# First experts: the bias row loaded once as 64 bytes a partition and spread over the rows by a VectorE transpose

## The reference, cut to what matters

```
u   = xb @ w1[e] + b1[e]                  # xb [rows, 1024], w1 [1024, 2048], b1 [2048]
glu = min(u[:, 0::2], 7)
lin = clip(u[:, 1::2], -7, 7)
act = glu * sigmoid(1.702 * glu) * (lin + 1)
y   = act @ w2[e] + b2[e]                 # w2 [1024, 1024]
```

## Time and profile before

| | us |
|---|---|
| median of 3 runs | 2942.95 |
| lowest, highest | 2941.94, 2943.54 |
| profiled execution | 2945.77 |
| its span on the core | 2944.0 |

### The profile page before, as it was taken

How to read it: one execution, slowest core, us unless ns; L and a number is a source line. 1 busy time by engine, 2 the same in 40 slices (tenths; PEclk the granted TensorE clock), 3 DMA queues, 4 the chain that set the end, 5 groups by cost and what they waited for, 6 DMA issues and landing times. The chain is left out here.

```text
span 2944.0 us, 49984 instructions
## 1 busy us (share of the span) xinstructions
PE 2274.4 (77%) x21092; PEld 1351.8 (46%) x21092; DVE 1044.5 (35%) x1860; ACT 741.9 (25%) x1812; POOL 116.7 (4%) x135
## 2 busy tenths in 40 slices
PE   4978798579999988888889946994897377574781
PEld 3944366424433333333333415884564246463660
DVE  2244554412222211122122224225565764543114
ACT  3123454111111101001011102223565414321231
POOL 0000000000000000000000010000000111000001
PEclk8988799779999999899999967997998588795995
DMA  5256501189999999999999943210000000303973
GB/s 213 97 228 218 233 1 65 60 343 364 370 406 395 401 404 402 401 399 401 396 399 400 405 165 139 99 37 5 1 1 1 1 1 8 122 15 152 417 294 116
DMA packets 148324, 631.12 MB, mean 214 GB/s; under 512 B 30788, under 2 KB 62532, under 8 KB 94856
## 3 DMA queue, kind: packets, MB, share of 16 engines
q1 hardware_dynamic: 118584, 580.48, 50.4%
q0 software_dynamic: 8352, 30.41, 2.8%
q10 hardware_dynamic: 21168, 17.06, 1.8%
HBM read 593.55 MB, written 34.37 MB: 213 GB/s over the span
## 5 line engine op out<-in xcount | busy, mean ns | idle before, releaser
L2024 PE MATMUL psum<-w,x 128*32 128x512 f32 x5696 | 674.9, 623 | 124.7 <-DMA w<-in_w_mlp 112.3
L2024 PEld LDWEIGHTS psum<-w,x 128*32 128x32 f32 x5696 | 183.3, 113 | 553.2 <-issue 398.3
L2175 DVE TENSOR_TENSOR u<-psum,x 128x512 f32<-128x512 f32 x89 | 61.5, 691 | 824.0 <-PE psum L2024 824.0
L2033 PE MATMUL psum<-w,act_turned 128*32 128x256 f32 x5696 | 330.8, 385 | 3.9 <-DVE act_turned L2184 3.6
L731 PE MATMUL psum<-high 128*128 128x512 f32 (+3 forms) x832 | 292.6, 352 | 36.9 <-DVE low L753 36.9
L731 PE MATMUL psum<-high,low 128*128 128x512 f32 (+3 forms) x832 | 291.4, 350 | 0.0
L731 PE MATMUL psum<-low,high 128*128 128x512 f32 (+3 forms) x832 | 291.3, 350 | 0.0
L2033 PEld LDWEIGHTS psum<-w,act_turned 128*32 128x32 f32 x5696 | 189.7, 112 | 174.3 <-issue 70.7
L753 DVE TENSOR_TENSOR low<-weight_slots,high 128x1024 fp32r<-128x1024 f32 (+3 forms) x84 | 89.2, 1066 | 290.9 <-ACT high L747 290.6
L731 PEld LDWEIGHTS psum<-high 128*128 128x128 f32 x832 | 159.7, 192 | 58.2 <-ACT high L747 37.7
L731 PEld LDWEIGHTS psum<-high,low 128*128 128x128 f32 x832 | 159.6, 192 | 20.1
(11 more groups left out here) (459 smaller groups left out, 2716.5 us busy)
## 6 DMA issues: line engine op xcount, KB each, us to landing
w<-in_w_mlp SPq DMA_DIRECT2D x192, 2048.0 KB, 30.0
weight_slots<-in_w_ada SPq DMA_DIRECT2D x12, 2048.0 KB, 10.8
weight_slots<-in_w_mod SPq DMA_DIRECT2D x12, 2048.0 KB, 10.9
weight_slots<-in_w_in SPq DMA_DIRECT2D x9, 2048.0 KB, 8.4
gu<-in_w_gate SPq DMA_DIRECT2D x16, 1024.0 KB, 12.7
gu<-in_w_up SPq DMA_DIRECT2D x16, 1024.0 KB, 15.5
down<-in_w_down SPq DMA_DIRECT2D x16, 1024.0 KB, 16.9
weight_slots<-in_w_out SPq DMA_DIRECT2D x6, 2048.0 KB, 11.0
```

Source lines behind the costliest of these rows:

```text
L2024: mm = pe.matmul(psum[g * RB:(g + 1) * RB, bank, :], b.turned[:, kc, q * RB:(q + 1) * RB], w[:, i, g * BANK:(g + 1) * BANK], start=kc == 0 ...
L2033: mm = pe.matmul(psum[g * RB:(g + 1) * RB, 2 + parity, 0:YW], b.act_turned[:, parity, kc, :], w[:, i, g * YW:(g + 1) * YW], start=kc == 0, ...
L2175: step.reach(dve.tensor_tensor(b.u[:], psum[:, bank, :], b.bias[:, parity], ALU.add), s.biased, at + 1)
```

## The change

The bias row of 8 KB is loaded by one DMA as 16 numbers (64 bytes) on each of the 128 partitions (`bias_in`, two small buffers by the turn's parity, and a third, `bias_in_over`, for the loop). When a turn begins, VectorE spreads it: one transpose instruction reads each number 32 times (a broadcast view) and writes 128x512 numbers, so that partition 32g+r gets the 512 numbers of slice g. There is one spread buffer instead of two. SP's wait ahead of the bias load is now for the spread of turn t-2 (`bias_spread`), not for the last addition of that turn. VectorE waits for weight piece 0 and the bias before the spread, once in a turn, and no more before each addition. In the loop the spread stands ahead of the wait for TensorE's first product.

```diff
--- before.py
+++ after.py
@@ -1906,7 +1906,8 @@
     YW = D // Q
     half = BANK // 2
     RING = 11
-    LOADS = per + Q
+    LOADS = per + 1
+    BC = BANK // RB
     turns = len(ranks)
     blocks = [(turn, i) for turn in range(turns) for i in range(by_rank[ranks[turn]])]
     n = len(blocks)
@@ -1923,10 +1924,11 @@
     freed = [done[last_of[j // per], j % per] for j in range(turns * per - RING, turns * per + per - RING)]
     freed = [max(freed[:c + 1]) for c in range(per)]
     homes = {"rows": k.x[:, 0], "turned": k.x[:, 1].rearrange("p (m q) -> p m q", q=P),
-             "bias": k.x[:, 2].rearrange("p (a n) -> p a n", a=2), "y": k.x[:, 3].rearrange("p (q n) -> p q n", q=Q)}
+             "bias": k.x[:, 2, 0:BANK], "bias_in": k.x[:, 2, BANK:BANK + 2 * BC].rearrange("p (a n) -> p a n", a=2),
+             "bias_in_over": k.x[:, 2, BANK + 2 * BC:BANK + 3 * BC], "y": k.x[:, 3].rearrange("p (q n) -> p q n", q=Q)}
     with buffers(core, others=homes, w=[P, RING, KU * 2 * FF1], u=[P, BANK], glu=[P, half], lin=[P, half],
                  sig=[P, half], act=[P, half], act_turned=[P, 2, DC, RB], slot_ids=[P, 1, I32]) as b, \
-            stage(core, "experts1", *[f"landed{a}_{c}" for a in range(2) for c in range(per)], "used", "biased",
+            stage(core, "experts1", *[f"landed{a}_{c}" for a in range(2) for c in range(per)], "used", "bias_spread", "biased",
                   "clipped", "squashed", "act_ready", "y_kept", "x_turned", "x_kept", "y_stored", "vector_step",
                   pool_dma=("gathered", "slots_free", "over_landed", "ids_made", "taken")) as (block, s):
         landed = [[s.landed0_0, s.landed0_1, s.landed0_2, s.landed0_3, s.landed0_4, s.landed0_5],
@@ -1934,13 +1936,13 @@
 
         def wait_landed(engine, turn, c):
 
-            engine.wait_ge(landed[turn % 2][c], 16 * (1 + Q * (c == 0)) * (turn // 2 + 1))
+            engine.wait_ge(landed[turn % 2][c], 16 * (1 + (c == 0)) * (turn // 2 + 1))
 
         def over_count(engine):
             return engine.value_load(r.n_over[0:1, 0:1], min_val=1, max_val=OVER1)
 
-        def bias_of(e, g):
-            return on_all(args.b_mlp1[0][ds(e, 1), g * BANK:(g + 1) * BANK], RB)
+        def bias_of(e):
+            return args.b_mlp1[0][ds(e, 1)].rearrange("a (p n) -> (a p) n", p=P)
 
         def weights_of(e, c):
             if c < UC:
@@ -1960,10 +1962,8 @@
                     if c == 0:
                         if turn >= 2:
 
-                            sync.wait_ge(s.biased, last_of[turn - 2] + 1)
-                        for g in range(Q):
-                            sync.dma_start(b.bias[g * RB:(g + 1) * RB, turn % 2], bias_of(e, g))\
-                                .then_inc(landed[turn % 2][0], 16)
+                            sync.wait_ge(s.bias_spread, turn - 1)
+                        sync.dma_start(b.bias_in[:, turn % 2], bias_of(e)).then_inc(landed[turn % 2][0], 16)
                     src = weights_of(e, c)
                     sync.dma_start(b.w[:, j % RING].rearrange("p (k n) -> p k n", k=src.shape[1]), src)\
                         .then_inc(landed[turn % 2][c], 16)
@@ -1979,10 +1979,9 @@
                     sync.dma_start(b.w[:, (turns * per + c) % RING].rearrange("p (k n) -> p k n", k=src.shape[1]), src)\
                         .then_inc(s.over_landed, 16)
 
-                sync.wait_ge(s.biased, i + n)
+                sync.wait_ge(s.bias_spread, i + turns)
                 sync.sem_inc(s.taken, 1)
-                for g in range(Q):
-                    sync.dma_start(b.bias[g * RB:(g + 1) * RB, 0], bias_of(e, g)).then_inc(s.over_landed, 16)
+                sync.dma_start(b.bias_in_over[:], bias_of(e)).then_inc(s.over_landed, 16)
 
         @block.gpsimd
         def _(pool):
@@ -2171,8 +2170,13 @@
         def _(dve):
             step = Steps(dve, s.vector_step)
 
-            def activate(at, bank, parity):
-                step.reach(dve.tensor_tensor(b.u[:], psum[:, bank, :], b.bias[:, parity], ALU.add), s.biased, at + 1)
+            def spread_bias(turn, columns):
+
+                step.reach(dve.transpose(b.bias[:].rearrange("p (j k) -> p k j", k=BC), spread(columns, 2, RB)),
+                           s.bias_spread, turn + 1)
+
+            def activate(at, bank):
+                step.reach(dve.tensor_tensor(b.u[:], psum[:, bank, :], b.bias[:], ALU.add), s.biased, at + 1)
                 step.reach(dve.tensor_scalar(b.glu[:], b.u[:, 0::2], LIMIT, None, ALU.min), s.clipped, at + 1)
                 step(dve.tensor_scalar(b.lin[:], b.u[:, 1::2], LIMIT, -LIMIT, ALU.min, ALU.max))
                 step(dve.scalar_tensor_tensor(out=b.lin[:], in0=b.lin[:], scalar=1.0, in1=b.glu[:], op0=ALU.add,
@@ -2185,10 +2189,12 @@
                     .then_inc(s.act_ready, 1)
 
             for at in range(n):
-                turn, _ = blocks[at]
+                turn, i = blocks[at]
+                if i == 0:
+                    wait_landed(dve, turn, 0)
+                    spread_bias(turn, b.bias_in[:, turn % 2])
                 dve.wait_ge(s.used, done[at, UC - 1])
-                wait_landed(dve, turn, 0)
-                activate(at, at % 2, turn % 2)
+                activate(at, at % 2)
                 if at >= 2:
 
                     dve.wait_ge(s.used, done[at - 2, per - 1])
@@ -2198,10 +2204,12 @@
             dve.wait_ge(s.act_ready, n)
             with dve.Fori(0, more) as i:
                 step.restart()
-                dve.wait_ge(s.slots_free, i * per + (per + UC))
                 dve.wait_ge(s.over_landed, i * (16 * LOADS) + 16 * LOADS)
                 dve.sem_inc(s.taken, 1)
-                activate(i + n, 0, 0)
+                spread_bias(i + turns, b.bias_in_over[:])
+                dve.wait_ge(s.slots_free, i * per + (per + UC))
+                dve.sem_inc(s.taken, 1)
+                activate(i + n, 0)
 
                 dve.wait_ge(s.y_kept, i + n)
                 dve.sem_inc(s.taken, 1)
```

## The result

| | before | after |
|---|---|---|
| median, us (5 runs each) | 2942.95 | 2878.46 |
| lowest to highest | 2937.65 to 2948.72 | 2876.99 to 2881.02 |
| ratio, with its 95% interval | | 0.9761 (0.9743 to 0.9779) |
| span of the profiled execution | 2944.0 | 2876.7 |

The direction was right and the size wrong.

The account below looks back on a forecast made before the run. The prediction took the DMA engines to bound the kernel from 755 us on. Its terms, 17.6 + 1.5 + 2.0 = 21.1 us, were rounded to 22, taking the median from 2942.95 to 2921 us, with a range of 2912 to 2933.

Parts of the forecast that it names:

- part 1: Bias loads: fewer bytes and smaller packets save 0.63 us a turn over 28 loads, 17.6 us; bounds 8.7 to 21.6.
- part 2: Stage start: one bias issue instead of four lets weights begin earlier, 1.5 us; bounds 0 and 2.1.
- part 3: Around 745 to 755 us: bias and next weight piece issued before the addition, saving 2.0 us; bounds 0 and 4.8.
- part 4: VectorE's spread, taken as 1.3 us a turn, lies hidden in its 5.83 us gap before the addition: no cost.
- The upper bound: Bias loads before the change: a fifth more for packets among long transfers, 0.84 us a turn, 21.6 us in all.
- the prediction's signs of being wrong: DMA share below 0.98 within 760 to 1680 us, rate under 395 GB/s there, or an addition released by the spread.
- (a): Rival: small bias packets cost more among large ones; saving 12.2 us, so 2931; chance 0.16.
- (c): Rival: a 64-byte packet costs more than the 2 KB one did; at 168 ns 15 us slower, 2958; chance 0.03.
- (b): Rival: TensorE becomes the bound in part of the stage, up to about 1000 us, losing 6.4 us: 2927; chance 0.12.
- (d): Rival: the bias bytes are not what fills the queue; only part 2 and part 3 stay, or less: 2939 to 2943; chance 0.05.

Follow-up runs that it names:

- one_dma_same: Kernel before, but a turn's bias is one DMA of 2 KB to each of 128 partitions, all from the same 2 KB; 2906.72 us, stage 1095.3 us.
- one_dma_own: Kernel before, but a turn's bias is one DMA over 128 partitions from 128 different 2 KB rows; 2911.69 us, stage 1092.2 us.
- old_wait: Kernel after, but SP waits ahead of the bias load for the last addition of turn t-2 as before; 2882.70 us, stage 1074.9 us.
- spread4: Kernel after, but the transpose that spreads the bias is done four times each turn instead of once; 2881.52 us, stage 1071.6 us.
- four_cols: Kernel before, but the four bias DMAs split columns, each writing 512 bytes to all 128 partitions; 2911.77 us, stage 1098.6 us.

## Why the prediction was wrong

The stage became 1135.5 - 1070.5 = 65.0 us shorter (means of two profiles each). The runs divide it so:

| part | predicted, us | measured, us | from |
|---|---|---|---|
| bytes and packets of the bias (part 1) | 17.6 | 18.9 | mean of one_dma_same and one_dma_own (1093.8) less old_wait (1074.9) |
| start (part 2), outside the stage measure | 1.5 | 1.5 of issue time; its effect on the end was not tested | bias to first weight issue: 2.05 before, 0.57 after (592.40 to 592.97) |
| earlier load (part 3) | 2.0 | 4.3 | old_wait twice, after twice |
| spread on VectorE (part 4) | 0 | 0 | spread4 |
| shape of the load: slowing of the weight packets, and of the bias's own | not in the sum | 41.7 | 1135.5 less 1093.8; the weight packets alone 40.4 (1000.1 less 959.7) |

- **The step that failed** is part 1's, where a load of the bias was priced by its own packets: "in a turn 0.67 us of all engines", from a window in which large loads of weights ran alone. 83.8 ns was the right price for a packet of a 128-partition load (85 ns in one_dma_same and one_dma_own); in the kernel before the bias packets took 99.9 ns, 0.80 us a turn, which is just the fifth more that the upper bound allowed. The price of the small ones was near (8.1 ns from the idle window, 11 ns in the full queue). What it put at nothing is what these packets do to the weight packets: 41.7 us of the stage, nearly twice the whole forecast. The upper bound (0.84 us a turn) allowed a fifth for the mixture and was itself the wrong kind of bound, since it let only the bias's own packets get slower.
- The rate of 402 GB/s was read as the ceiling of the queue. A view of windows of 4 us, or the GB/s line of a shorter stretch, would have shown 333 beside 423 at the same share, and that the dips follow the bias loads. The page of the whole span has slices of 73.6 us, in which two turns are averaged away.
- What bounds the kernel was right: DMA time saved after 755 us is end time, up to the loop, where TensorE still waits 8.17 us for the bias load's landing. Part 3 was half of what was measured, inside its bounds. Part 4 was right in its cover; the spread itself takes 1009 ns, not twice the transpose of half its size (1.3 us).
- None of the prediction's signs of being wrong appeared: the DMA share stays at 1.01 or 1.02 in each stretch from 760 to 1600 us, the rate doesn't fall under 395 GB/s, and no addition is released by the spread. All of them looked for a smaller gain; none was set for a larger one.
- Rivals: (a) and (c) fall, by the packet time of 11 ns. The trace of the kernel before could have told it: the 4-byte completions of SP's queue took 10.3 ns each in this stage, small packets under load. The Trainium skill's rule on transfers under 512 B (DMA: Bandwidth & Descriptors, section Specifications) agrees with the trace in that line rate is not reached: 64 B in 11 ns are 5.8 GB/s an engine. A price of the size that (c) needed is not there. (b) falls: in the kernel after, TensorE is busy for 200.00 of the 200 us from 800 to 1000, but the DMA share is 1.01 there, so nothing was given back. (d) was the opposite of what happened: the bytes were not the whole of what filled the queue, but what else filled it went with them.
- The range came out too narrow because all cases of a faster kernel shared the same premise, that a transfer takes from the queue its own packets' time and no more.

## What to carry to other kernels

In a stage bound by DMA, compare GB/s at the same DMA share in windows shorter than one period of the loop: a share of 1 with a rate that dips says that some transfer slows its neighbours, and its removal is then worth more than its bytes (here 42 us on top of 19). Look at the destination's partitions first: loads of 2 KB packets into 32 partitions, or into 0 to 63, were dear in this full queue, and cut along the free dimension or spread over 128 partitions they were not. The shape is worth more here than the bytes: the runs that only changed it (one_dma_same, one_dma_own, four_cols, all of which load wrong numbers) already had 37 to 42 of the 65 us. Where an engine has idle time, as VectorE had, it can do the replication and save the bytes too.

## What the runs showed of the hardware that was not expected

- 64 packets of 2 KB into partitions 0 to 63 a turn cost 21.8 us of stage more than the same into partitions 32 to 95 (1103.4 against 1081.6 us; 410 against 422 GB/s).
- The weight packets in the neighbourhood of the 32-partition loads took 43.5 to 45.9 ns a KB in place of 39, for about 13 us, while the bias packets themselves filled 0.80 us of the engines. That it lasts so long fits the 12 us over which a turn's bias packets are spread among the others; in one_dma_same they are spread over as long (11.6 us), and nothing slows. Why so few packets slow all others is not settled: that engines queue at the ports reached would fit, but no view shows a port.
- ScalarE's stores of `y`, which read from 32 partitions each, have no such effect in the kernel after: the rate there never dips under 413 GB/s in slices of 12.5 us, though such stores run after every fourth block, and in the first 12 us after a store's first packet the weight packets take 38.5 to 38.6 ns a KB, no more than elsewhere.
